# Nine of eleven down blocks with 2x2 block sums: seven products of 256 columns for the left half

## The reference

```python
def _swiglu(h, w_gu, w_down):
    g, u = jnp.split(h @ w_gu, 2, axis=-1)
    return (jax.nn.silu(g) * u) @ w_down

x = x + 0.5 * _rmsnorm(_swiglu(_rmsnorm(x, ffn1_pre_g), ffn1_w_gu, ffn1_w_down), ffn1_post_g)
...
x = x + 0.5 * _rmsnorm(_swiglu(_rmsnorm(x, ffn2_pre_g), ffn2_w_gu, ffn2_w_down), ffn2_post_g)
```

## Time and profile before

| | us |
|---|---|
| median of 3 runs | 1080.8 (1080.31 to 1081.05) |
| the profiled execution | 1081.31 |
| its span, first to last instruction | 1079.4 |
| TensorE busy | 1068.7 (99%) |
| VectorE busy | 789.1 (73%) |
| ScalarE busy | 608.5 (56%) |

### The profile page before, as it was taken

One profiled execution on the slowest core, in us unless ns is written; L12 is line 12 of the kernel. 1 busy time (PEld: TensorE's weight loads), 2 busy tenths in 40 slices (PEclk: granted clock), 3 DMA queues, 4 the chain that ended last, 5 costly groups with the idle time before them and its releaser, 6 DMA issues.

```text
span 1079.4 us, 21082 instructions
## 1 busy us (share of the span) xinstructions
PE 1068.7 (99%) x8534; PEld 1009.7 (94%) x8534; DVE 789.1 (73%) x1125; ACT 608.5 (56%) x905; POOL 0.2 (0%) x4
## 2 busy tenths in 40 slices
PE   9999999999999999999999999999999999999999
PEld 7999999999989999999999998999999799999898
DVE  5665556989979777778778555775655887997884
ACT  5544444678586545878445556444444575655471
POOL 0000000000000000000000000000000000000000
PEclk9999999999999999999999999999999999999999
DMA  9866556465543454444546533465556355542251
GB/s 343 292 213 211 176 182 209 151 221 174 179 154 121 152 181 157 157 164 149 208 166 244 196 106 130 147 230 198 188 182 212 119 177 200 191 157 95 102 196 39
DMA packets 29297, 190.71 MB, mean 177 GB/s; under 512 B 3656, under 2 KB 4521, under 8 KB 7466
## 3 DMA queue, kind: packets, MB, share of 16 engines
q1 hardware_dynamic: 26480, 182.53, 48.6%
q10 hardware_dynamic: 2746, 7.16, 1.9%
HBM read 188.62 MB, written 1.05 MB: 176 GB/s over the span
## 4 chain that ended last, share of the span: by engine, by line
PE 87%; DVE 9%; ACT 2%; issue 1%; DMA 1%; SPq 0%; DVEq 0%; ACTq 0%
PE bank L526 15%; PE bank L528 15%; PE bank L527 15%; PE bank L538 10%; PE bank L539 10%; PE bank L540 10%; DVE sb_w_lo L2098 3%; PE bank L625 2%; PE bank L761 1%; DVE sb_ssd_conv L2409 1%; DMA sb_w_raw<-in_w 1%; PE bank L709 1%; PE bank L886 1%; ACT sb_w_hi L1371 1%; PE bank L1048 1%
## 5 line engine op out<-in xcount | busy, mean ns | idle before, releaser
L2098 DVE TENSOR_TENSOR sb_w_lo<-sb_w_raw,sb_w_hi 128x2048 fp32r<-128x2048 f32 x169 | 386.4, 2289 | 118.9 <-ACT sb_w_hi L1371 118.5
L1371 ACT ACTIVATE sb_w_hi<-sb_w_raw 128x2048 fp32r<-128x2048 f32 x169 | 322.9, 1911 | 33.0 <-PE bank L528 29.2
L526 PE MATMUL bank<-sb_hT_hi,sb_w_hi 128*128 128x256 f32 (+1 forms) x816 | 225.7, 277 | 0.0
L528 PE MATMUL bank<-sb_hT_hi,sb_w_lo 128*128 128x256 f32 (+1 forms) x816 | 225.7, 277 | 0.0
L527 PE MATMUL bank<-sb_hT_lo,sb_w_hi 128*128 128x256 f32 (+1 forms) x816 | 225.6, 276 | 0.0
L538 PE MATMUL bank<-sb_hT_hi,sb_w_hi 128*128 128x256 f32 (+2 forms) x744 | 213.1, 286 | 0.2 <-DVE sb_hT_lo L2175 0.2
L539 PE MATMUL bank<-sb_hT_lo,sb_w_hi 128*128 128x256 f32 (+2 forms) x744 | 206.2, 277 | 0.0
L540 PE MATMUL bank<-sb_hT_hi,sb_w_lo 128*128 128x256 f32 x744 | 205.9, 277 | 0.0
L526 PEld LDWEIGHTS bank<-sb_hT_hi,sb_w_hi 128*128 128x128 f32 (+1 forms) x816 | 152.7, 187 | 0.0
L528 PEld LDWEIGHTS bank<-sb_hT_hi,sb_w_lo 128*128 128x128 f32 (+1 forms) x816 | 152.6, 187 | 0.0
L527 PEld LDWEIGHTS bank<-sb_hT_lo,sb_w_hi 128*128 128x128 f32 (+1 forms) x816 | 152.6, 187 | 0.0
(11 more groups left out here) (516 smaller groups left out, 2077.9 us busy)
## 6 DMA issues: line engine op xcount, KB each, us to landing
sb_w_raw<-in_w SPq DMA_DIRECT2D x169, 1024.0 KB, 4.9
sb_w_raw<-in_w SPq DMA_DIRECT2D x4, 512.0 KB, 7.8
sb_hT<-in_xT SPq DMA_DIRECT2D x2, 512.0 KB, 5.3
sb_x<-in_x SPq DMA_DIRECT2D x2, 512.0 KB, 11.8
sb_mem_xn<-in_mem ACTq DMA_DIRECT2D x1, 1024.0 KB, 7.1
sb_mem_T<-in_memT ACTq DMA_DIRECT2D x1, 1024.0 KB, 10.4
sb_post_g<-in_ffn_post_g ACTq DMA_DIRECT2D x2, 512.0 KB, 5.7
sb_decay<-in_c_decay ACTq DMA_DIRECT2D x1, 768.0 KB, 5.3
```

The lines of the kernel that those rows point to most:

```text
L526: pe.matmul(o, a_hi, b_hi, start=first, stop=False)
L528: return pe.matmul(o, a_lo, b_hi, start=False, stop=last)
L1371: act.activation(w_hi[b % STAGES][:], w_raw[b % RING][:], ACT.Copy).then_inc(w_hi_in, 1)
L2098: tt(w_lo[b % STAGES][:], w_raw[b % RING][:], f32(w_hi[b % STAGES][:]), ALU.subtract).then_inc(w_lo_in, 1)
```

## The change

Down blocks 1 to 9 of each part ("mixed" blocks) no longer compute the left 512 output columns by eight products. Write the activations of the pair as four 128 x 128 tiles (hidden tile by token half) and the left weights as four tiles of 256 columns. Their product is a 2 x 2 block product, done by seven products of 256 columns of sums of tiles. The right 512 columns stay four plain products of 512, in banks 7 and `last_bank`. Down blocks 0 and 10 stay plain.

- **Weights.** The host reorders the columns of a mixed block: the right halves first, then the four left tiles. VectorE makes three sums of weight tiles (`mix_block`) before ScalarE's rounding, ScalarE rounds them too (768 columns), VectorE makes `mix_lo`.
- **Activations.** VectorE makes four sums of 128 columns (`first_sum` behind the even tile, `other_sums` after the odd tile's `act`), ScalarE rounds them (`sums_high`, 512 columns), VectorE makes `sum_lo`.
- **Banks.** The seven products go to banks 3, 4 (shared with the plain blocks), 5 and 6. Banks 5 and 6 are opened by a product on zeros: bank 6 at the start of the kernel, bank 5 of part one and both of part two before the last product of down block 0. Up blocks use two banks in turn; `up1.2` uses bank 5.
- **End.** After down block 9 ScalarE copies bank 5 and VectorE joins the sums (`join`) into a tile `joined`; at the end the banks of the plain products are added to it (two additions of 512 columns), and the squares and gains of the left half read `joined`.
- **Others.** The transpose for the memory's norm moves from before up block 20 into its middle; the spectra use banks 5 and 6.

```diff
+MIXED_OF = {down_at(n, c): MIXED_PAIRS * (n - 1) + c - 1 for n in (1, 2) for c in range(1, PAIRS - 1)}
...
+            def open_mixed(n, q):
+
+                claim(f"mixed{n}.{q}", 5 + q, down_at(n, PAIRS - 2))
...
+                down_banks = (3, 7, 4, last_bank)
+
+                def up_bank(j):
+
+                    return 5 if n == 1 and j == 2 else (FIRST[f"ffn{n}"] + j % 2) % 3
...
+                def mixed_block(c, turn=0, parts=(512,), all_three=False):
...
+                    tile_in(c, 0, turn)
+                    plain_half(banks[7], 0, top)
+                    tile_in(c, 1, turn)
+                    plain_half(banks[7], 1, top)
+                    of_tile(5, 0, 0, top, hi, lo, b11, False)
+                    of_tile(3, 0, 1, top, hi, lo, b21, False)
+                    of_tile(4, 0, 1, low, mix_hi, mix_lo, u4, False)
+
+                    pe.wait_ge(S("ffn_sum_lo"), MIXED_PAIRS * (n - 1) + c + turn)
+                    of_sum(3, 1, 3, hi, lo, b22, False)
+                    of_sum(5, 1, 0, mix_hi, mix_lo, u1, True)
+                    of_sum(6, 0, 1, hi, lo, u2, False)
+                    of_sum(6, 1, 2, mix_hi, mix_lo, u3, True)
+                    plain_half(banks[last_bank], 0, low)
...
+                            if first and k and i == 3:
+                                pe.wait_ge(S("zero_r"), n)
+                                for q in range(n):
+                                    open_mixed(n, q)
+                                    pe.matmul(banks[5 + q][:], zero_r[:], hi[:, 0, 0:512], start=True, stop=False)
...
             stay_warm(zeros[:, 0:P], zeros[:], 1)
+            open_mixed(1, 1)
+            pe.matmul(banks[6][:], zeros[:, 0:P], zeros[:], start=True, stop=False)
             ffn_part(1, 0)
...
+                if b in MIXED_OF:
+
+                    act.wait_ge(S("ffn_mixed"), MIXED_OF[b] + 1 + turn)
+                    act.activation(w_hi[b % STAGES][:], w_raw[b % RING][:], ACT.Copy)
+                    act.activation(mix_hi[:], mix_raw[:], ACT.Copy).then_inc(w_hi_in, 1)
...
+                def join():
+
+                    wait_read(dve, f"mixed{n}.0")
+                    y, p5, w = f["joined"], f["parts"][:, 0, :], f["parts"][:, 1, :]
+                    o = full(dve, f"mixed{n}.1")
+                    link(tt(w, o[:, 0:256], y[:, 0, 0:256], ALU.subtract))
+                    link(tt(y[:, 0, 256:512], w, p5, ALU.add))
+                    tt(y[:, 1, 0:256], o[:, 256:512], w, ALU.subtract)
+                    read(tt(y[:, 1, 256:512], y[:, 0, 256:512], o[:, 256:512], ALU.subtract), f"mixed{n}.1")
...
+                        if j % 2:
+                            other_sums(j // 2, turn)
+                    for b in behind:
+                        if b in MIXED_OF:
+                            mix_block(b, turn)
                     for b in between:
                         if steps:
                             steps.pop(0)()
...
+                    if mixed:
+                        (sums_low if j % 2 else first_sum)(j // 2, turn)
...
+                if n == 1:
...
+                    dve.wait_ge(S("zeros"), 1)
+                    tt(zero_r[:], zeros[:, 0:P], zeros[:, 0:P], ALU.subtract).then_inc(S("zero_r"), 1)
...
+                    join()
                     hidden_tile(FF_TILES - 1, [], [b + 2], 0, [mem_lows])
...
                     hidden_tile(FF_TILES - 1, [], [])
+                    join()
```

More of the change, by code:

```diff
@@ L739, in up_block, with tile_in, last_product @@
                     feature_products(o, b, 2, hT_hi, hT_lo, key=f"up{n}.{j}").then_inc(block_done, 1)
-                def down_block(c, turn=0, parts=(512,), all_three=False):
+                def tile_in(c, k, turn):
+                    pe.wait_ge(S("ffn_lo"), FF_TILES * (n - 1) + 2 * c + 1 + k + 2 * turn)
+                def last_product(o, w_hi, w_lo, parts, all_three):
+                    t = slice(P, SEQ)
+                    for m, (a, w) in enumerate(((f["hi"], w_hi), (f["hi"], w_lo), (f["lo"], w_hi))):
+                        at = 0
+                        for width in parts if all_three or m == 2 else (512,):
+                            mm = pe.matmul(o[:, at:at + width], a[:, 1, t], w[:, at:at + width], start=False, stop=False)
+                            at += width
+                    return mm
@@ L746, in down_block, with plain_block @@
+                def plain_block(c, parts=(512,), all_three=False):
+                    b = down_at(n, c)
+                    first, last = c == 0, c == PAIRS - 1
+                    pe.wait_ge(w_lo_in, b + 1 - SPLIT_FROM)
                     hi, lo = halves(b, 2, D)
+                    if first:
+                        for i in range(4):
+                            claim(f"down{n}.{i}", down_banks[i], down_at(n, PAIRS - 1) if i == 3 else None)
                     for k in range(2):
-                        pe.wait_ge(S("ffn_lo"), FF_TILES * (n - 1) + 2 * c + 1 + k + 2 * turn)
@@ L764, in down_block @@
+                            if last and k == 1 and i < 3:
                                 ends(mm, f"down{n}.{i}")
```

161 lines of the change are left out of this document (121 added, 40 removed).

## The result

The kernel before takes 1080.7 us (median of 4 runs, 1080.3 to 1081.1), the changed one 1088.8 us (median of 4, 1088.4 to 1091.9): a ratio of 1.0081 with a 95% interval of 1.0062 to 1.0100, so it is slower by 0.8%. The forecast was 1088.0, between 1084.5 and 1093.5. The profiled execution has a span of 1086.6 us against 1079.4. (So the two profiles lie 7.2 us apart and the medians 8.1: the profiled execution of the changed kernel was the fastest of its four, 1088.4, and that of the kernel before, 1081.3, lay above all four of its own.)

What follows compares the result with a forecast made beforehand. TensorE, busy 1068.7 of 1079.4 us, bounds steady turns; VectorE sets the parts' openings and ends. Part one +4.0, part two +2.85 and start +0.3 make 7.15 us: 1088.0 as a median, range 1084.5 to 1093.5.

Steps and rivals of the forecast that it cites:

- saving per mixed block: TensorE, each mixed down block: 5.24 us instead of 5.49, saving 0.25 us, eighteen times 4.5.
- steady turns: Feed-forward loop: TensorE stays the bound at 16.14 us against VectorE's 15.7, so the additions cost nothing there.
- wait at bank 5: Part one's opening: TensorE's zero product waits 2.2 us until tile 2's `act` has read bank 5.
- `join` at tile 21's gate, added: End of part one: `join` adds 1.6 us ahead of a gate that waited 0.96, so 0.65.
- additions of 512, added: End of part one: two VectorE additions (2 x 0.61) before the squares, less 0.3 of waits for squares: 1.0 us.
- part two, opening, to the first turn's end: TensorE waits 0.6 and 0.65 us for VectorE's low parts of the weights; 1.6 us late at the first turn's end.
- transposes behind it: After part two's residual: 0.2 us less, since half of `x` was done 0.2 before TensorE's transposes start.
- start: Kernel start: one more fp32 zero product opens bank 6 and runs 0.6 to 0.9 later, worth half: +0.3 us.
- slower pace of up blocks: Rival: up blocks stay at the slow pace, 0.2 us each, some 14 before each end; 1093.5 us, chance 0.13.
- early clock: Rival: at the start the full clock rises as the first block begins, 1.6 us come back; 1086.4 us, chance 0.15.
- The ends cost nothing: Rival: VectorE's additions behind down block 8 (some 4.3 us per part) run in its idle time; 1077.3 us, chance 0.05.
- Nothing lost or gained: Rival: one end is hidden or the opening waits fall away, 3 to 4 us less; 1082 to 1083 us, chance 0.05.

Runs made afterwards that it cites:

- e12: Changed kernel with the joining of the sums left out (join's additions and the two of 512 columns cut to 2 columns, output wrong); ratio 1.0048 to the kernel before.
- e5: Changed kernel with the last of the nine mixed blocks, down block 9 of each part, plain again; ratio 1.0055 to the kernel before.
- e2: Changed kernel with part one's zero product on bank 5 moved into the middle of the next up block; ratio 1.0087 to the kernel before.
- e8: Changed kernel with fold_difference and fold_sum in part two's opening each moved behind a low part of the weights; ratio 1.0087 to the kernel before.

## Why the prediction was right, step by step

| step | forecast, us | measured, us |
|---|---|---|
| saving per mixed block | 0.25 | 0.20 |
| steady turns | no wait | none; VectorE's own turn 15.85 (15.7 forecast) |
| wait at bank 5 | 2.2 (34.55 - 32.5, its own numbers, is 2.05) | 2.03 |
| late at the up block of 55.11 | 2.6 | 2.6 |
| late when down block 8 ends | 0.9 | 1.1 |
| tile 19's gate, added | 0.55 | 0.67 |
| sums and `sum_hi`, added | 1.0 | 1.00 |
| `join` at tile 21's gate, added | 0.65 | 0.41 |
| additions of 512, added | 1.0 | 0.75 |
| part one | +4.0 | +3.9 |
| part two, opening, to the first turn's end | 1.6 (its own terms give 1.45) | 1.65 |
| part two, end of down block 8 | -0.15 | +0.3 |
| part two, from there to the residual | 3.2 | 3.1 |
| transposes behind it | -0.2 | 0.0 |
| part two | +2.85 | +3.43 |
| start | +0.3 | not told from 0 |
| sum | 7.15 | 7.2 |

The mechanism and its places were right, and part of the agreement in size is luck: VectorE's added work costs nothing in the turns and its full length where VectorE is already last. VectorE's own turn of 15.85 can be read off its low parts:

```profile
97.60 2.29 DVE L2200 TENSOR_TENSOR sb_w_lo<-sb_w_raw,sb_w_hi 128x2048 fp32r<-128x2048 f32 x1 [1.12 <-ACT sb_w_hi L1459]
...
113.44 2.29 DVE L2200 TENSOR_TENSOR sb_w_lo<-sb_w_raw,sb_w_hi 128x2048 fp32r<-128x2048 f32 x1 [1.11 <-ACT sb_w_hi L1459]
```

After the opening it runs behind TensorE and catches up 0.34 us a turn; the cover of 0.4 us that I gave the additions was real, and thin.

The mis-sized term is the saving. I took 118 ns for a product of 256 and the fast pace for the products of 512. They ran at 119.6, and five of nine of the 512s took 231 to 236 ns instead of 227; a block takes 5.29 us, not 5.24. In the sum this counts in the seven turns of each part: they gave back 1.50 and 1.35 us where 1.75 each was forecast, 0.65 us that did not come. By the Trainium skill's formula (the same page and section) a block would save 0.30, an estimate; the measured 0.20 decides against it, and the slower rows of before were the better guide. This miss was paid for by terms that I had put 0.2 to 0.3 too high: `join` in part one, the additions of 512, the start. Part two shows it bare: of the 0.58 us by which it exceeds the forecast, 0.40 is the saving and 0.2 the wait at the transposes.

The opening of part two came out near its 1.6 by luck. Its terms, 0.45 for the zero products, 0.6 and 0.65 of waits less 0.25, make 1.45. Measured are 0.49 for the products, 0.52 at the first wait and some 0.4 at the second, less the same 0.2; the missing 0.43 had arisen before the first down block, in the up block that ran at 123 ns a product from 686.4 us on (115.7 before), and no term of mine has it. Why that block became slower stays open. In the same way the end of part one needed VectorE and ScalarE to have caught up by down block 8, which I took from the turns before the change; they had, by 0.13 us.

Of the rivals, the slower pace of up blocks did not come (113.5 ns in every steady turn). The early clock came and was worth nothing, because I had priced it on TensorE alone; its next wait, in front of the first down block, took it in. "The ends cost nothing" is out by e12 and e5. "Nothing lost or gained" needed bank 5 read earlier; e2 removed that wait and gained nothing.

## What to carry to other kernels

Trading products on TensorE for additions on another engine pays only where that engine waits; read its slack at the opening and the end of a loop, not in the turn, and multiply by what the exchange costs there. When two waits overlap, removing either brings little or nothing, so try both together. A step may stand inside a wait of its own engine and be all but free there; look for that before you move it (e8). And an engine that is made to wait in one long pause instead of several short ones may come back at half its clock: look at the granted clock behind every pause that an edit lengthens.
